# Four engines run the eight head groups of the gated recurrent mixer in hardware loops instead of written out, and one engine's list of weight splits is shifted by a step

## The reference

```python
q, i_in, f_fw, f_bw, z = split(h @ w_in, 5)            # w_in: 1024 x 10240
log_f = logaddexp(log(lb), log1p(-lb) + log_sigmoid(gf)) # for both directions
k = (1 - lb) * sigmoid(-gf)
# per head, in time:  S = exp(log_f) * S + k v^T ;  o = q S
o = forward(silu(q), k_f, i_in, log_f) + backward(...)
y = (rmsnorm(o) * silu(z)) @ w_out
```

## Time and profile before

| | |
|---|---|
| median of 3 runs | 1783.98 us (1783.55 to 1785.29) |
| time of the profiled execution | 1785.29 us |
| its span | 1783.2 us |
| PE matmuls | 1719.9 us busy, 96% of the span |
| PE weight loads | 1530.5 us, 86% |
| DVE | 1207.0 us, 68% |
| ACT | 901.2 us, 51% |
| the seven groups of the layer that overlap with a next one | 918 to 1429 us of the span |

### The profile page before, as it was taken

How to read it: one execution, slowest core, us unless ns; L and a number is a source line. 1 busy time by engine, 2 the same in 40 slices (tenths; PEclk the granted TensorE clock), 3 DMA queues, 4 the chain that set the end, 5 groups by cost and what they waited for, 6 DMA issues and landing times.

```text
span 1783.2 us, 35713 instructions
## 1 busy us (share of the span) xinstructions
PE 1719.9 (96%) x15070; PEld 1530.5 (86%) x15070; DVE 1207.0 (68%) x1673; ACT 901.2 (51%) x1096; POOL 44.4 (2%) x47
## 2 busy tenths in 40 slices
PE   6999999998999999999999999999999989999998
PEld 5877799987987789988888898898988967899896
DVE  5888755546678865545557768668677785577874
ACT  5564543335475443334645446455454553466772
POOL 2000000000000000000000000000000000000130
PEclk9999999998999999999999999999999999999999
DMA  8558568654457566655322222222212122352112
GB/s 197 189 189 299 150 169 198 189 190 147 147 180 270 204 165 185 184 193 179 86 85 72 73 72 73 74 71 84 72 61 84 61 96 95 113 169 69 49 60 106
DMA packets 254734, 238.28 MB, mean 134 GB/s; under 512 B 32288, under 2 KB 217680, under 8 KB 254320
## 3 DMA queue, kind: packets, MB, share of 16 engines
q1 hardware_dynamic: 253440, 233.21, 42.3%
q0 software_dynamic: 1136, 2.81, 0.6%
HBM read 234.94 MB, written 1.05 MB: 132 GB/s over the span
## 4 chain that ended last, share of the span: by engine, by line
PE 82%; DVE 6%; ACT 4%; DMA 3%; DVEq 2%; issue 1%; ACTq 1%; SPq 1%
PE pg L2540 35%; PE pg L1246 34%; PE pm L1246 7%; PE pm L2540 2%; PE pm L1249 2%; DMA ring<-in_ada_w 1%; DMA ring<-in_w_in 1%; DVE ring_r L567 1%; DMA ring<-in_hg_w_in 1%; PE pm L2543 1%; ACT ring_r L560 1%; DVEq L1734 1%; DVE ring L1732 1%; DVE ring_r L1698 0%; SPq L2163 0%
## 5 line engine op out<-in xcount | busy, mean ns | idle before, releaser
L567 DVE TENSOR_TENSOR ring_r<-ring,ring_r 128x2048 fp32r<-128x2048 f32 (+1 forms) x126 | 283.5, 2260 | 153.0 <-ACT ring_r L560 147.4
L1246 PE MATMUL pg<-ring_r,work_r 128*128 128x256 f32 (+3 forms) x1792 | 381.0, 324 | 4.5 <-DVE work_r L1704 3.4
L2540 PE MATMUL pg<-ring_r,work_r 128*128 128x512 f32 (+1 forms) x1776 | 379.3, 373 | 5.3 <-DVEq L3012 2.9
L2540 PEld LDWEIGHTS pg<-ring_r,work_r 128*128 128x128 f32 x1776 | 307.8, 190 | 68.6 <-issue 8.4
L1246 PE MATMUL pg<-ring_r 128*128 128x256 f32 (+3 forms) x1008 | 329.0, 326 | 2.5 <-DVEq L779 1.4
L1246 PEld LDWEIGHTS pg<-ring_r,work_r 128*128 128x128 f32 x1792 | 300.8, 190 | 29.9 <-DVEq L1699 3.4
L2540 PE MATMUL pg<-work_r,ring_r 128*128 128x256 f32 x2688 | 318.8, 281 | 5.9 <-DVEq L3002 3.1
L2540 PEld LDWEIGHTS pg<-work_r,ring_r 128*128 128x128 f32 x2688 | 317.4, 188 | 7.4 <-DVE ring_r L567 3.7
L560 ACT ACTIVATE ring_r<-ring 128x2048 fp32r<-128x2048 f32 (+1 forms) x126 | 237.2, 1890 | 167.8 <-DMA ring<-in_w_ffn_up 69.4
L1246 PE MATMUL pg<-work_r,ring_r 128*128 128x512 f32 (+1 forms) x976 | 263.9, 360 | 0.0
L1246 PEld LDWEIGHTS pg<-ring_r 128*128 128x128 f32 x1008 | 191.6, 190 | 17.6 <-DVEq L779 1.6
(11 more groups left out here) (380 smaller groups left out, 1854.9 us busy)
## 6 DMA issues: line engine op xcount, KB each, us to landing
ring<-in_hg_w_in SPq DMA_DIRECT2D x80, 512.0 KB, 4.0
ring<-in_w_in SPq DMA_DIRECT2D x36, 1024.0 KB, 5.1
ring<-in_ada_w SPq DMA_DIRECT2D x24, 1024.0 KB, 7.0
ring<-in_w_ffn_gate SPq DMA_DIRECT2D x44, 512.0 KB, 3.9
ring<-in_w_ffn_up SPq DMA_DIRECT2D x44, 512.0 KB, 5.3
ring<-in_w_ffn_down SPq DMA_DIRECT2D x22, 1024.0 KB, 4.8
ring<-in_w_out SPq DMA_DIRECT2D x12, 1024.0 KB, 4.9
ring<-in_ple_w_gate SPq DMA_DIRECT2D x8, 1024.0 KB, 4.8
```

The source lines that it names most:

```text
L567: W.low_done(V.tensor_tensor(lo, W.raw(i, name)[:, 0:lo.shape[1]], W.hi(i, name).bitcast(f32), ALU.subtract))
L1246: return T.matmul(out_, lhsT, rhs, start=first, stop=last)
L2540: return T.matmul(out_, lhsT, rhs, start=first, stop=last)
```

## The change

`all_groups` gets the engine as an argument. Group 0 is still called once. Groups 1 to 4 become a hardware loop `eng.Fori(0, 2)` whose body holds two groups (the `b` = 1 and the following `b` = 0 one), and groups 5, 6 and 7 stay written out. PE, ACT and DVE do this each in its own stream. SP's loop over `n` becomes a hardware loop of four rounds with the 20 DMAs of two groups in its body. Inside a loop `n` is a register. So the value that a wait compares with is computed by register instructions, the DRAM address of a weight DMA comes from a register, and the one ACT instruction that writes `oT[g]` has a register in its address. Each loop ends in a compare-and-branch back to its head. The trip count is fixed: PE, ACT and DVE branch back once, SP three times.

Apart from that, `lows` on DVE is shifted. The low part of gb0 is made after level 1 and not after level 0, gb1 after 2 and not 1, q0 after 3 and not 2, q1 and v0 after 4 and not 3, v1 after 5 and not 4. This holds for all groups.

```diff
-        def all_groups(group):
-
-            for g in range(NG):
-                group(*divmod(g, 2), divmod(g + 1, 2) if g + 1 < NG else None, divmod(g + 2, 2) if g + 2 < NG else None, g - 1 if g else None)
+        def all_groups(eng, group):
+
+            group(0, 0, (0, 1), (1, 0), None)
+            with eng.Fori(0, NG // 2 - 2) as n:
+                group(n, 1, (n + 1, 0), (n + 1, 1), n * 2)
+                group(n + 1, 0, (n + 1, 1), (n + 2, 0), n * 2 + 1)
+            n = NG // 2 - 2
+            group(n, 1, (n + 1, 0), (n + 1, 1), n * 2)
+            group(n + 1, 0, (n + 1, 1), None, n * 2 + 1)
+            group(n + 1, 1, None, None, n * 2 + 2)
...
-            for n in range(NG // 2):
+            with sp.Fori(0, NG // 2) as n:
...
-                HM.release(A.activation(dst[:, g, :], HM.buf("oT"), ACT.Copy, scale=p_ogain), "oT")
+                dst = dst[:, g, :] if isinstance(g, int) else dst[:, bass.ds(g, 1), :].rearrange("p a n -> p (a n)")
+                HM.release(A.activation(dst, HM.buf("oT"), ACT.Copy, scale=p_ogain), "oT")
...
-            all_groups(group)
+            all_groups(act, group)
...
-            all_groups(group)
+            all_groups(pe, group)
...
-                lows = (("gf1", "gb0"), ("gb1",), ("q0",), ("q1", "v0"), ("v1",), (), ())
+                lows = (("gf1",), ("gb0",), ("gb1",), ("q0",), ("q1", "v0"), ("v1",), ())
...
-            all_groups(group)
+            all_groups(dve, group)
```

## The result

The changed kernel takes 1800.6 us, the median of four runs (1798.85 to 1801.1), against 1783.76 for the kernel before in the same comparison. The ratio is 1.0093, with a 95% interval of 1.0081 to 1.0105: 16.6 us slower, by 14 to 19. The forecast was 1798, range 1790 to 1805. The profiled executions have spans of 1801.2 and 1783.2 us, so 18.0 apart, and the traces account for these 18.0.

A forecast was written before the change was run, and what follows sets the result against it. PE was taken to bound the layer, with only 2.3 us of waits to gain. Shift 8.2, DVE registers 1.6, PE registers 1.0, branch 2.7 and chain 0.4 made 13.9 us: 1799.2 profiled, median 1798, range 1790 to 1805.

The forecast's parts named there:

- The shift: Units 5 and 6, groups 0 to 6: PE waits for late low parts of q1 and v1, 7 x 1.17 = 8.2 us.
- rival 4: Waits at units 5 and 6 add up, as PE's delay at q1 delays DVE's level 5: +3, 1801 us; chance 0.08.
- DVE's registers: Register instructions on DVE's path to v1's low part: 0.4 us in each of the loop's four groups, +1.6.
- The branch: PE's branch back after group 3's level-0 burst: code fetch 2.0 + 1.0 = 3.0 us, 2.7 net, bounds 0 to 5.0.
- the sum: All terms over the profiled execution of 1785.3 us: 8.2 + 1.6 + 1.0 + 2.7 + 0.4 = 13.9 us, giving 1799.2.
- the 1.4 for PE's registers and for the chain at a group's start: Two terms: 1.0 us for PE's register instructions, 0.4 for SP's and ACT's lengthening the chain at three group boundaries.
- DVE's branch at nothing: DVE's branch back priced at nothing, because DVE is ahead of PE by more than a microsecond.
- PE's registers: 100 register instructions in PE's loop, mostly hidden behind running matmuls, perhaps exposed at level bursts: +1.0 us, bounds 0 to 12.
- Rival 2: Registers are exposed on PE, at level bursts: 5 to 12 us in place of 1.0, 1802 to 1809 us; chance 0.11.
- The 0.4 for SP's and ACT's registers: Their register instructions lengthen the weight-DMA chain at three group boundaries by 0.1 to 0.2 us each: +0.4.
- Rival 1: PE's branch costs only its issue, next instructions already on their way: sum 11.2 us, time 1795; chance 0.20.
- Rival 3: DVE's idle time swallows the shift, v1's low part is in time: 1782 to 1785 us with a hidden branch; chance 0.09.

The follow-up runs named there:

- experiment 1: The kernel before, written out, with only the list of low parts shifted as in the changed kernel: ratio 1.0041, 7.3 us slower.
- 4: The kernel before, written out, with the shifted list except that q1's low part stays after level 3: ratio 0.9999, no difference.
- 5: The kernel before, written out, with the shifted list except that v1's low part stays after level 4, as third there: ratio 1.0043, 7.7 us slower.
- 7: The changed kernel with the unshifted list and PE written out, loops only on DVE, ACT and SP: ratio 1.0004, 0.7 us slower.
- 9: The changed kernel's loops with heads placed at a packet's start, without the hint; single run, no ratio given, stop at PE's branch 5.3 us.
- 2: The changed kernel with the unshifted list of low parts, so loops on all four engines alone: ratio 1.0042, 7.5 us slower.
- experiment 6: The changed kernel with the unshifted list and a loop on PE only, the other three engines written out: ratio 1.0044, 7.9 us slower.
- experiment 10: The kernel before plus five PE loops of useless matmuls, 13 to 166 KB, the fifth hinted; no ratio given, branches 0.21 to 3.60 us.
- experiment 3: The changed kernel with the unshifted list and a branch prefetch hint in the loops of PE, DVE and ACT: ratio 1.0037, 6.6 us slower.
- 8: The changed kernel with the unshifted list, hinted loops and each loop's head at the start of a 16 KB packet: ratio 1.0009, 1.6 us slower.
- 12: The changed kernel with hint, heads placed at a packet's start, and q1's low part kept after level 3: ratio 1.0024, 4.3 us slower than before.

## Why the prediction was right, and where it was not

**The shift: right, in mechanism and size.** The working gave 1.17 a group from rows of one group; written out (experiment 1) the measured loss is 1.18. Its inner account holds as well, q1 first (0.35 measured, 0.4 forecast) and v1 with the rest (0.83), not added on top, so rival 4 is out. That level 4's second low part is the cause is shown twice: take it away and the loss is gone (4), add a third and level 5 loses on its own (5).

**DVE's registers: right, a little high.** Forecast 0.4 a group in four groups; the groups of the loop lose 0.3 more than those outside it, and level 4 is 0.28 longer beyond the low part. Shift and these together: 9.8 forecast, 9.8 measured. They cost only because DVE is late there: with the old list they cost nothing (7).

**The branch: the mechanism right, the size too small.** This is the step that failed: "PE waits for one issue-to-landing", priced "2.0 + 1.0 = 3.0", 2.7 with the wait absorbed, upper bound 5.0. It measured 6.6 and lies outside its bounds, for two reasons. The stop is 4.9 to 5.4 in the four traces without the hint, with two packets of code in three of them and one in the fourth (9); what holds PE there before the last packet starts, 2.5 to 2.7 us into the stop, is not shown for the whole of that time. And the price of the clock was left out: 1.49 us net, for matmuls at half of it. This term alone is 3.9 too small, nearly all of the 18.0 - 13.9 = 4.1 that the sum was short of the profiled span. The forecast for the median was 2.6 short. Luck is in this: the 1.4 for PE's registers and for the chain at a group's start is near the 1.2 that the trace has outside of units 5 and 6 and the branch, but the cause given for it is not what was found.

That PE comes to the head of a long body without its code at hand is what experiments 2, 6 and 10 agree on. In 2 and 6 two packets of code start in the stops of 4.9 and 5.4 us. A body of 51 KB, over three packets of 16 KB, is branched back in 0.21 us with no packet, and one of 115 KB in 3.35 to 3.60 us with one: a body of 800 instructions does not pay, one of 1800 does, and what lies between was not measured. PE's own loop runs 3803 instructions in a round.

**DVE's branch at nothing: right only under cover.** The prediction called DVE "ahead of PE by more than a microsecond". It stood for 3.6 us behind its branch. What hid this was PE's own stop; without it (7) it costs 1.9 in the trace.

**PE's registers: next to nothing.** Forecast 1.0, measured 0.2 in experiment 6. Rival 2 is out. The 0.4 for SP's and ACT's registers at the starts of three groups was not found either: with these in loops and PE written out (7) the starts of groups 1, 2 and 4 are 0.00 longer. The changed kernel has 0.08, 0.74 and 0.00 there. Rival 1 is out by the stop of 5.16. It holds for short bodies alone: their branches took 0.21 to 0.24 in experiment 10, and cost PE nothing there (0.213 a matmul with the branch in it, as in the longer bodies). Rival 3, DVE gaining from the shift, is out: its level 4 is tied to PE's burst (the gap there grew to 1.68), as the argument against it had said.

**Left open.** The intervals between bursts 1 and 5 are some 0.04 longer each in the changed kernel and in experiments 1, 3 and 4, and for the most part not in 2, 5, 7 and 8, so neither shift nor loops explain this microsecond. DVE's stop of 1.7 to 2.3 us in group 5 comes in all three kernels with hint and placement, and neither with the hint alone (3) nor with the placement alone (9). Each time an 8 KB packet of code had landed 1.5 to 1.6 us before DVE went on; why this packet comes so late is not shown. Why a weight DMA at a group's start takes now 3.9, now 5.3 to 5.6 us was not tested.

## What to carry to other kernels

When work is moved to a later step, count what stands in each step of the engine that does it, not how late the moved piece may be: here five pieces could move at no cost, and the sixth cost 1.2 us a group because it was second in its step. A loop in hardware cost PE nothing while its body was held (51 KB). With bodies of 115 and 166 KB its sequencer stopped for 3.3 to 3.6 us at each branch back, and in this kernel, with 3803 instructions in a round, PE stood for 4.9 to 5.4 without the hint. In the changed kernel 1.5 us for the lower clock behind the stop came on top. With the hint and the head at a packet's start the branch itself cost 0.55, but the entry cost 1.2 to 1.8 once, and new stops appeared behind the loop. The other way, to put the branch behind long matmuls that PE has queued, follows from experiment 10 and was not tried in this kernel.

## What the runs showed of the hardware

- The granted clock is 0.50 or 1.00 in every trace; a value between is the mean of a stretch (before: 1.00 in 430 to 435 us, 0.50 in 436 to 440). PE's was 0.50 behind the stop of 5.16 us, 0.71 as the mean of the 3 us behind one of 3.3 us (experiment 3), and 0.54 in 997 to 1000 us behind one of 1.82 us (12). Behind one of 1.22 us (8) and behind waits of 0.45 and 0.90 us (1256 to 1268 us of the changed kernel) it was 1.00. In the four traces with stops of 4.9 to 5.4 us the interval with the stop is 6.2 to 7.7 longer.
- In the loops of experiment 10 the granted clock is 0.50 at every branch, although PE had a matmul under way in all of that time (3.50 of 3.50 us in the row above).
- In the changed kernel the branch back was taken without a stop on ACT (0.05 us, next instruction 0.21 later) and on SP (0.05 us), and with one of 3.6 us on DVE, which runs 326 instructions in a round where ACT runs 215 and SP 98. In experiments 3, 8 and 9 DVE's next instruction came 0.3 us after its branch began.
- PE's trace of the changed kernel has 50 register instructions in a round, 40 `ALU_OP` (0.03 to 0.04 us each) and 10 `FUSED_REGOPS` (0.04 to 0.06). The listings of the program ahead of the prediction have them as `REGISTER_ALU` and `ISA`.
- The 1 + 31 matmuls that the program has for a level burst are 64 in the trace, where PE's rows have them as x64.
- The hint brings PE's stop from 4.9 to 3.1 us where the head is not placed (3), and to 0.4 where it stands at the start of a packet (8) (records of the branch instruction, 4.86, 3.14 and 0.40). In experiment 10 0.4 was reached without placing the head.
